# Attention of a fused two-block kernel: one pass per tile with a late combination, against two passes with the groups' weights put onto the exponents

## What is computed

```python
DILATION_CFG = ((128, 1), (512, 4), (2048, 16))

def dilated_window_attention(q, k, v, window, dilation):
    ...
    scores = jnp.where(valid[None, :, None, None], scores, -jnp.inf)
    m = jnp.max(scores, axis=-1, keepdims=True)
    p = jnp.exp(scores - m)
    den = jnp.sum(p, axis=-1)
    o = jnp.einsum('bnrhij,bnjrhd->bnirhd', p, vv)
    ...

def mixing_sublayer(h, cos, sin, w_in, w_pool, b_pool, pool_scale, w_out):
    ...
    alpha = jax.nn.softmax(jnp.stack(lses, axis=0), axis=0)
    attn = jnp.sum(alpha[..., None] * jnp.stack(outs, axis=0), axis=0)
    attn = attn.reshape(B, S, ATTN_OUT_WIDTH).astype(h.dtype)
    pool = causal_multiscale_pool(u_pool, w_pool, b_pool, pool_scale)
    return jnp.concatenate([pool, attn], axis=-1) @ w_out
```

## Time and profile before

| | |
|---|---|
| median of 3 runs | 1703.22 us (1702.44 to 1706.0) |
| the profiled execution, its own time | 1704.47 us |
| its span, first to last instruction | 1702.7 us |
| granted TensorE clock, mean | 0.957 |
| busy PE, PEld, DVE, ACT, POOL | 92%, 74%, 36%, 39%, 42% of the span |
| last transpose of the keys (end of the projection) | starts at 185.95 us |
| unit 10 of the output projection | starts at 277.69 us |

### The profile page before, as it was taken

One profiled execution on the slowest core, in us unless ns is written; L12 is line 12 of the kernel. 1 busy time (PEld: TensorE's weight loads), 2 busy tenths in 40 slices (PEclk: granted clock), 3 DMA queues, 4 the chain that ended last, 5 costly groups with the idle time before them and its releaser, 6 DMA issues.

```text
span 1702.7 us, 19973 instructions
## 1 busy us (share of the span) xinstructions
PE 1567.0 (92%) x7680; PEld 1264.1 (74%) x7680; DVE 610.5 (36%) x960; ACT 670.4 (39%) x1013; POOL 713.1 (42%) x608
## 2 busy tenths in 40 slices
PE   7899757799999999999988898999989999999996
PEld 4699534678888888878865567787878788887885
DVE  3665364433333300134024431243234455655001
ACT  2542452454444422332234354453333554554231
POOL 0466100344455444464421135334534445555442
PEclk8999886799999999999999998999999999999999
DMA  8463201512222233223311122222222222222221
GB/s 363 170 251 138 86 1 26 125 64 99 99 89 83 77 102 93 100 78 103 129 37 38 37 99 100 75 74 86 88 79 71 74 99 85 88 99 81 93 84 65
DMA packets 27148, 162.82 MB, mean 96 GB/s; under 512 B 3240, under 2 KB 3368, under 8 KB 12360
## 3 DMA queue, kind: packets, MB, share of 16 engines
q1 hardware_dynamic: 23616, 151.01, 25.9%
q10 hardware_dynamic: 3464, 10.88, 2.5%
HBM read 157.15 MB, written 4.72 MB: 95 GB/s over the span
## 4 chain that ended last, share of the span: by engine, by line
PE 68%; issue 10%; POOL 8%; DVE 7%; DMA 3%; ACT 3%; POOLq 0%; SPq 0%; ACTq 0%; DVEq 0%
PE ps L1624 58%; POOL WL L703 7%; DMA adaw<-w_ada_dram 2%; PE ps L1590 1%; PE ps L1835 1%; DMA raw<-w_up_dram 1%; PE ps L1849 1%; PE ps L1862 1%; DVE S L1515 1%; ACT S L906 1%; POOL WL L667 1%; DVE ps L1217 1%; PE ps L1789 1%; DVE S L1502 1%; DVE xT L1222 1%
## 5 line engine op out<-in xcount | busy, mean ns | idle before, releaser
L667 POOL TENSOR_TENSOR WL<-raw,WH 128x512 fp32r<-128x512 f32 (+2 forms) x344 | 368.9, 1101 | 621.0 <-ACT WH L783 620.9
L1624 PE MATMUL ps<-hH,WH 128*128 128x512 f32 x1136 | 461.1, 406 | 24.8 <-POOL hL L681 8.9
L1624 PE MATMUL ps<-hL,WH 128*128 128x512 f32 x1136 | 454.1, 400 | 0.0
L1624 PE MATMUL ps<-hH,WL 128*128 128x512 f32 x1136 | 453.9, 400 | 0.0
L703 POOL TENSOR_TENSOR WL<-raw,WH 128x512 fp32r<-128x512 f32 x176 | 246.2, 1431 | 254.1 <-ACT WH L931 254.1
L1624 PEld LDWEIGHTS ps<-hH,WH 128*128 128x128 f32 x1136 | 216.7, 191 | 83.6 <-issue 29.3
L1624 PEld LDWEIGHTS ps<-hH,WL 128*128 128x128 f32 x1136 | 216.5, 191 | 52.9
L1624 PEld LDWEIGHTS ps<-hL,WH 128*128 128x128 f32 x1136 | 216.9, 191 | 50.5
L783 ACT ACTIVATE WH<-raw 128x1024 fp32r<-128x1024 f32 (+3 forms) x172 | 148.1, 885 | 235.0 <-PE ps L1624 231.3
L1624 PE MATMUL ps<-hidH,WH 128*128 128x512 f32 x352 | 137.9, 392 | 1.1 <-POOL WL L703 1.1
L1624 PE MATMUL ps<-hidL,WH 128*128 128x512 f32 x352 | 137.0, 389 | 0.0
(11 more groups left out here) (269 smaller groups left out, 2268.4 us busy)
## 6 DMA issues: line engine op xcount, KB each, us to landing
raw<-w_up_dram SPq DMA_DIRECT2D x44, 1024.0 KB, 4.9
raw<-w_in_dram SPq DMA_DIRECT2D x36, 1024.0 KB, 4.9
adaw<-w_ada_dram SPq DMA_DIRECT2D x20, 1024.0 KB, 7.2
raw<-w_down_dram SPq DMA_DIRECT2D x16, 768.0 KB, 4.2
raw<-w_down_dram SPq DMA_DIRECT2D x16, 640.0 KB, 3.9
adap<-w_ada_dram SPq DMA_DIRECT2D x4, 1024.0 KB, 18.2
xT<-x_dram ACTq DMA_DIRECT2D x2, 2048.0 KB, 10.8
raw<-w_mem_kv_dram SPq DMA_DIRECT2D x4, 1024.0 KB, 4.8
```

The lines of the kernel that those rows point to most:

```text
L667: pool.tensor_tensor(WL[:, d % 2, ks, cols], raw[:, d % 2, ks, cols], WH[:, d % 2, ks, cols].bitcast(F32), ALU.subtract).then_inc(lo_done, 1)
L1624: mm = pe.matmul(out, lhs[x], rhs[y], start=(first and i == 0), stop=(last and i == 2))
```

## The change

The attention is rearranged into two passes.

First pass: all tiles' scores and exponents. Tiles 0 to 4 stand in the list between the projection's units 8 and 9 and their halves, the rest behind it. The mask is no longer added by DVE: TensorE puts it into the bank first, as a product of an fp32r identity with a mask table, and adds the scores to it. Tiles use two pairs of banks in turn, (4, 5) and (6, 7). DVE takes the maxima from PSUM. For tiles 5, 7, 9 and 11 (`WHOLE_EXP`) DVE then subtracts the maximum from all four heads at once, ACT takes one exponent of 512 elements, and DVE sums it (`tile_sum`); for the others ACT takes four exponents from PSUM with their sums. All exponents stay in `S1`.

Then the weights: maxima and sums stand with the queries on partitions, 48 of each. Those of group 0 (`md0`, contiguous queries) are brought into the order of the other groups by a store to DRAM and a load, and group 0's weights go back the same way (`al0`), four small transfers on SP's queue. DVE multiplies each tile's exponents with its weights (`scale`), first the eight tiles of groups 1 and 2, then group 0.

Second pass: 15 key blocks (`SUM_BLOCKS`), each four transposes, an ACT copy and four products with `V1`, all added up in banks 4 and 5 from a start of zeros. The steps `combine` and the copies to `oT` and `stats` are gone; the result is cut into `hH` and `hL` from PSUM (`attn_out`). The ACT and DVE part of `pool` is now `pool_out`, after key blocks 3 and 7. The cut of unit 11 (`split`) is behind the weights. Below are the tables, the list, the helpers, and then SP, ACT, DVE and TensorE.

```diff
 TILES1 = [(g, b, 2 if g == 0 and b > 0 else 1) for g in range(GROUPS) for b in range(TT)]
+NEAR = TT
+WHOLE_EXP = (5, 7, 9, 11)
+SCORE_BANKS = [((4, 5), (6, 7))[i] for i in (0, 1, 0, 0, 1, 0, 1, 0, 1, 0, 1, 0)]
+SUM_ORDER = list(range(NEAR, len(TILES1))) + list(range(NEAR))
+SUM_BLOCKS = [(n, kb) for n in SUM_ORDER for kb in range(TILES1[n][2])]
...
+            if d == ADA_REST:
+                steps += [("ada_end", 2)]
+            if d >= ADA_REST:
+                steps += [("front", 3 * (d - ADA_REST)), ("front", 3 * (d - ADA_REST) + 1)]
...
                 steps += [("trig",)]
             steps += [("seg", d, 1), ("evac_in", d)]
             if d == 3:
-                steps += [("spread_lo",)]
-            steps += [("split", d + 2)]
+                steps += [("spread_lo",), ("masks",)]
+            if d < D_OUT - 1:
+                steps += [("split", d + 2)]
+            if d == ADA_REST:
+                steps += [("front", 2)]
             if d < 3:
                 steps += [("spread_hi", k) for k in range(3 * d, min(3 * d + 3, KD))]
             if d in (1, 2, 4, 5):
...
-        steps += [("ada_end", 2), ("front", 0), ("pool",), ("front", 1)]
-        for n in range(len(TILES1)):
-            steps += [("mid", n)]
-            if n + 2 < len(TILES1):
-                steps += [("front", n + 2)]
-            steps += [("back", n)]
-        steps += [("combine",), ("bias_fetch",)]
+        steps += [("front", 5), ("pool",)] + [("front", n) for n in range(6, len(TILES1))] + [("weights",), ("split", D_OUT + 1)]
+        steps += [("scale", n) for n in SUM_ORDER] + [("mid", 0)]
+        for i in range(len(SUM_BLOCKS)):
+            if i + 1 < len(SUM_BLOCKS):
+                steps += [("mid", i + 1)]
+            steps += [("back", i)]
+            if i in (3, 7):
+                steps += [("pool_out", i // 4)]
+        steps += [("attn_out",), ("bias_fetch",)]
...
+        def scores(n):
+            nk, i = TILES1[n][2], key_blocks(n)
+            t = S1z[:] if n == len(TILES1) - 1 else S1[:, i:i + nk, :]
+            return t.rearrange("p k c -> p (k c)").rearrange("p (x w) -> p x w", x=GH)
+        def score_psum(n, x):
+            w = P * TILES1[n][2]
+            return ps[:, SCORE_BANKS[n][x // 2], w * (x % 2):w * (x % 2) + w]
+        def scores_read(eng, n):
+            if n in WHOLE_EXP:
+                eng.wait_ge(less_max, WHOLE_EXP.index(n) + 1)
+            else:
+                eng.wait_ge(exp_done, exps_before(n + 1))
...
-            dense(D_OUT, D_UP1)
+            dense(D_OUT, D_OUT + 3)
+            sp.wait_ge(negm_ready, NEAR)
+            sp.wait_ge(exp_done, exps_before(NEAR))
+            sp.dma_start(near_stats.ap().rearrange("(b p) c -> p b c", p=P), md0[:].rearrange("p b i h -> p b (i h)")
+                         ).then_inc(near_stored, 16)
+            sp.wait_ge(near_stored, 16)
+            sp.dma_start(mdj[:, 0, :, :, :].rearrange("p b i h -> p (b i h)"), near_stats.ap().rearrange("(p r) c -> p (r c)", r=TT)
+                         ).then_inc(near_loaded, 16)
+            sp.wait_ge(alpha_ready, 1)
+            sp.dma_start(near_weights.ap().rearrange("(p r) h -> p (r h)", r=TT), al[:, 0, :, :].rearrange("p b h -> p (b h)")
+                         ).then_inc(weights_stored, 16)
+            sp.wait_ge(weights_stored, 16)
+            sp.dma_start(al0[:], near_weights.ap().rearrange("(b p) h -> p b h", p=P)).then_inc(weights_loaded, 16)
+            load(D_OUT + 3)
...
             def front(n):
-                sc.wait_ge(negm_ready, n + 1)
-                w = P * TILES1[n][2]
+                t = scores(n)
+                if n == 0:
+                    sc.wait_ge(ada_turned, len(ADA_DVE))
+                if n in WHOLE_EXP:
+                    sc.wait_ge(less_max, WHOLE_EXP.index(n) + 1)
+                    sc.activation(t, t, ACT.Exp, scale=DH ** -0.5).then_inc(exp_done, 1)
+                    return
+                sc.wait_ge(negm_ready, n + 1 - sum(1 for i in WHOLE_EXP if i < n))
                 for x in range(GH):
-                    t = S1[:, n % 2, x // 2, x % 2, 0:w]
-                    sc.activation(t, t, ACT.Exp, bias=negm[:, n, x:x + 1], scale=DH ** -0.5,
...
+                    sc.activation(t[:, x, :], score_psum(n, x), ACT.Exp, bias=negm[:, n, x:x + 1], scale=DH ** -0.5,
+                                  accum_out=tile_stats(n)[:, 1, x:x + 1]).then_inc(exp_done, 1)
+            def weights():
                 sc.wait_ge(gap_ready, 1)
-                sc.activation(alpha[:], alpha[:], ACT.Exp, scale=DH ** -0.5).then_inc(gap_exp, 1)
-                for hp in range(2):
-                    sc.wait_ge(attn_ready, hp + 1)
-                    sc.activation(hH[:, 2 + hp, :], comb[:, 0, :], ACT.Copy).then_inc(cat_hi, 1)
+                sc.activation(al[:], al[:], ACT.Exp, scale=DH ** -0.5).then_inc(gap_exp, 1)
+            def mid(i):
+                sc.wait_ge(pt_done, i + 1)
+                if i >= 4:
+                    sc.wait_ge(pv_done, i - 3)
+                sc.activation(PT1[:, i % 4, :], ps[:, 6 + i % 2, :], ACT.Copy).then_inc(pt_read, 1)
+            def attn_out():
+                for q in range(2):
+                    sc.wait_ge(o_ready, q + 1)
+                    sc.activation(hH[:, 2 + q, :], ps[:, 4 + q, :], ACT.Copy).then_inc(cat_hi, 1)
...
+            def tile_sum(n):
+                ve.wait_ge(exp_done, exps_before(n + 1))
+                ve.tensor_reduce(tile_stats(n)[:, 1, :], scores(n), X, ALU.add).then_inc(far_summed, 1)
             def front(n):
+                nk = TILES1[n][2]
+                ve.wait_ge(s_done, 2 * n + 2)
+                top = tile_stats(n)[:, 0, :]
+                first, second = SCORE_BANKS[n]
+                src = ps[:, first:second + 1, 0:2 * P * nk].rearrange("p e (q w) -> p e q w", q=2)
+                link(ve.tensor_reduce(top.rearrange("p (e q) -> p e q", e=2), src, X, ALU.max))
+                if n in WHOLE_EXP:
+                    ve.tensor_tensor(scores(n).rearrange("p (e q) w -> p e q w", e=2), src,
+                                     top.rearrange("p (e q) -> p e q", e=2).unsqueeze(3).broadcast_to([P, 2, 2, P]), ALU.subtract
+                                     ).then_inc(less_max, 1)
+                else:
+                    ve.tensor_scalar(negm[:, n, :], top, -DH ** -0.5, None, ALU.mult).then_inc(negm_ready, 1)
+                if n - 1 in WHOLE_EXP:
+                    tile_sum(n - 1)
+            def weights():
+                tile_sum(WHOLE_EXP[-1])
+                ve.wait_ge(far_summed, len(WHOLE_EXP))
+                ve.wait_ge(near_loaded, 16)
+                top, total = mdj[:, :, :, 0, :], mdj[:, :, :, 1, :]
+                link(ve.tensor_reduce(mx[:], over_groups(top), X, ALU.max))
+                ve.tensor_tensor(al[:], top, over_all(mx[:]), ALU.subtract).then_inc(gap_ready, 1)
+                ve.wait_ge(gap_exp, 1)
+                link(ve.tensor_tensor(wt[:], al[:], total, ALU.mult))
+                link(ve.tensor_reduce(den[:], over_groups(wt[:]), X, ALU.add))
+                link(ve.reciprocal(rden[:], den[:]))
+                ve.tensor_tensor(al[:], al[:], over_all(rden[:]), ALU.mult).then_inc(alpha_ready, 1)
+                ve.wait_ge(alpha_ready, 1)
+            def scale(n):
...
+                if n == 0:
+                    ve.wait_ge(weights_loaded, 16)
+                w = al0[:, b, :] if n < NEAR else al[:, g, b, :]
+                ve.tensor_tensor(scores(n), scores(n), w.unsqueeze(2).broadcast_to([P, GH, P * nk]), ALU.mult).then_inc(p_scaled, 1)
+            def attn_out():
+                for q in range(2):
+                    ve.wait_ge(cat_hi, 3 + q)
+                    ve.tensor_tensor(hL[:, 2 + q, :], ps[:, 4 + q, :], hH[:, 2 + q, :].bitcast(F32), ALU.subtract
                                      ).then_inc(cat_lo, 1)
...
             def turn(e):
                 pe.wait_ge(rope_done, 2 * e + 2)
+                if e >= 4:
+                    scores_read(pe, (1, 4)[e - 4])
...
+                pe.wait_ge(turn_read, 12 if n >= 6 else 10 if n == 4 else 4 * g + 4)
+                if n == 0:
+                    pe.wait_ge(masks_ready, 2)
+                    pe.wait_ge(mod_ready, 3)
+                before = [i for i in range(n) if SCORE_BANKS[i] == SCORE_BANKS[n]]
+                if before:
+                    scores_read(pe, before[-1])
+                first = 0 if nk == 2 else 2 * P if g == 2 else P
+                for bank in SCORE_BANKS[n]:
+                    pe.matmul(ps[:, bank, 0:2 * P * nk], ident_r[:],
+                              mask[:, first:first + P * nk].unsqueeze(1).broadcast_to([P, 2, P * nk]), start=True, stop=False)
+                k0 = P * (b + 1 - nk)
                 for q in range(2):
                     for e in range(2):
                         r = slice(64 * e, 64 * e + 64)
-                        mm = pe.matmul(ps[:, 4 + e, 256 * q:256 * q + P * nk], qT[r, 2 * g + q, P * b:P * b + P],
```

(30 more changed lines are left out.)

199 lines of the change are left out of this document (61 added, 138 removed).

## The result

The changed kernel took 1665.99 us (median of 4, 1664.66 to 1666.63) against 1703.37 us in the runs beside it: a ratio of 0.9778, 95% interval 0.9763 to 0.9792. The forecast was 1662.5 us, range 1655 to 1680. The profiled execution has a span of 1664.8 us against 1702.7, so 37.9 us have to be found.

What follows compares the result with a forecast made beforehand. TensorE bounds the whole kernel, but in the attention no engine is full and dependent steps wait on each other. Unit 10 38.7 us earlier plus 2.0 behind it gives 40.7: 1662.5 us, range 1655 to 1680.

Steps and rivals of the forecast that it cites:

- What is added to the projection: Tiles 0 to 4 add 6.4 us on TensorE, the `ada_end` wait 0.8; last `turn` starts at 193.2.
- Tiles 5 to 11: Behind the projection: `pool` 3.6 us, paired tiles 3.5 us a round, last round 6.2; ends at 211.7.
- Weights: Between the passes: small DVE and ACT operations with hand-overs take 1.9 us; first `scale` ends at 214.3.
- rival 3: One unseen cost: strided PSUM writes, DVE slowed beside POOL, or slower PSUM exponents; +5 to +10, 1670 us; chance 0.15.
- Second pass: 15 key blocks at 1.12 us, 16.8, plus zeros 0.5, slow clock 2.5 and pool copies 3.0; ends at 237.2.
- the slow start: Start of the second pass: TensorE comes in at the lower clock after little work, losing 2.5 us.
- the pooled rows: In the second pass, `pool_out` work in ACT's way shows 1.5 us twice, 3.0 in all.
- Round trips: Four small DRAM transfers of weights, hidden at 2.3 us each; covers 21.4 and 13.1 us.
- Rival 4: DRAM transfers delay DVE and the second pass; 18.8 us each eats all 40.7, 19.7 gives 1707; chance 0.01.
- Behind it: After the attention, unit 10 runs at full clock, 2.0 us more gain; later waits move along.
- rival 2: TensorE stays at 1.2 GHz from tile 6 to unit 10: +17.8, 1680 us; chance 0.08.
- rival 1: First pass stays at full clock and pool copies hide: 4 to 6 less, 1658 us; chance 0.15.

Runs made afterwards that it cites:

- the fill: Thirteen unread TensorE products added between tile 11's scores and the weights, against the changed kernel: 1662.48 us.
- the run with seven: Six more DRAM round trips of the near groups' weights before the load `scale` waits for, against the changed kernel: 1680.18 us, ratio 0.9869.
- unchanged kernel: The changed kernel without a further edit, run in three groups: 1665.99, 1668.48 and 1664.61 us.

## Why the prediction was right, step by step

| step | forecast | measured (first profile) |
|---|---|---|
| last `turn` starts | 193.2 | 194.08 in the timeline |
| sum of tile 11 ends | 211.7 | 212.05 |
| first `scale` ends | 214.3 | 215.37 |
| second pass, with its waits | 22.9 us | 23.0 us |
| unit 10 starts | 239.0 | 240.30 |
| its first 24 products | 5.8 | 7.39 |

- **What is added to the projection.** Forecast 7.2, measured 8.1. The term that was mis-sized most is the mask products: from start to start in the timeline two of 256 columns take 0.40 to 0.43 where 0.24 was reckoned from the product of 512 in the earlier trace rows, two of 512 0.56 to 0.66 for 0.48, so 2.6 us for 1.9. (In the dense stretch two products of 256 columns take 0.24, so the pair by itself was priced rightly; where one kind of product gives way to another it costs more, and why, no run shows.) The wait for `ada_end` costs 1.1 us for 0.8 (from `ada_turn` to the next product 1.93, before 0.81); small pieces add 0.2, and this execution came to `ada_turn` 0.3 sooner. Halves of units 8 and 9 are 5.73 to 5.77 from start to start, as before (5.74), so the five tiles' other work is hidden there.
- **Tiles 5 to 11.** `pool` takes 1.86 where the earlier trace rows has 3.6: those were eight instructions at the lower clock (0.52 granted in 190 to 193.4 us of the trace before). That gives 1.7 back, and the clock, at 0.50 from 204 on, takes most of it: a tile's scores take 1.16 and 1.21 instead of 0.65 to 0.69. The forecast had the low clock only in the last tile. Its path at the end is not the measured one either: it has DVE's queue (sum of 9, maximum of 11, subtraction) behind tile 10, 6.2 us from tile 10's scores on; measured it is TensorE, whose scores of tiles 10 and 11 take 3.85 us one behind the other while DVE waits 0.40 for them, 6.7 us in all. The end was off by only 0.35 us because these cancel: +1.0 from the projection and tile 5, -1.7 from `pool`, +0.6 in the two rounds, +0.5 at the end.
- **Weights.** L1436 and the first `scale` were stretched beside GpSimd's cutting, 0.8 us (shown by moving it). It is the part of rival 3 that came true, at 0.8 and not 5 to 10 us. The other part did not: products of groups 1 and 2, which write every fourth column of PSUM, take 0.59 like those of group 0. The Trainium skill (SBUF — State Buffer, section "Door 1: The DMA port swizzle") says that any non-contiguous access to PSUM slows matmuls down significantly; here it doesn't, and the measurement decides.
- **Second pass.** 23.0 us for 22.9, of which the slow start is 2 (1.5 came back with the fill, DVE's second `scale` covers the rest) and the pooled rows 2.3 for 3.0 (shown by moving them). That the sum meets the forecast is luck: a key block takes 1.17 us where 1.12 was reckoned, 0.8 over the 15, and TensorE waits 0.19 before the last products; together that is about what the slow start and the pooled rows were too high by (0.3 to 0.5 and 0.7).
- **Round trips.** Four transfers landed in 1.4 to 1.8 us, the estimate was 2.3; no engine waited for them. Rival 4's mechanism is real, with its cover of 13.1 us measured as 13.4, but it needs more trips than one: in the run with seven the third already landed too late, at 229.96. The forecast took its risk from a load of 160 KB in 2.3 us and one at the start in 19.7; the case that matters here is a load beside x's, which took 7.75 (with its store 9.1, still inside the cover).
- **Behind it.** Here the one step fails: "TensorE was dense until 2 us before, so unit 10 should run at the full clock: 7.81 - 5.79 = 2.0 us more". It ran at 0.63 and 0.52 of the clock in 240 to 244 us, and 0.4 us was gained. The forecast's own sum has two gaps in this pass, so by its own terms TensorE was not dense; it was busy 84% of 222 to 238 us. The unchanged kernel had 7.39, 5.85 and 7.29 in three profiles, so the step is not wrong every time: the forecast took for certain what comes out one way or the other from execution to execution. The Trainium skill (TensorE: Matmul & The Clock Gate, section "HAM oscillation") has a kernel in which waits between bursts of matmuls bring the throttled level back again and again; the forecast priced that only as rival 2, for the whole stretch, and not for this one place. That such a fall can come behind 1.88 us without work, with two gaps of 1.17 us before, is what these traces show, in 5 of 6.
- **Sum.** 37.4 + 0.4 = 37.8 us for 38.7 + 2.0 = 40.7. The 1.3 us in unit 10's start are the 0.9 of the projection (most of it the mask products), and the 0.8 of GpSimd less what `pool` and the rest gave back; the 1.6 are the clock. The time of the whole kernel alone could not have judged such terms: two executions of the changed kernel took 1658.3 us, the number of rival 1, and the one of them that was profiled has the same stretch (45.90).

## What to carry to other kernels

Price a rebuilt stretch by one mark at its end and build the sum by pieces: the terms here were off by up to 1.7 us each, with both signs, and the sum by 2.9 of 40.7. When a chain of dependent steps per tile is taken apart into passes, look at three things: the operation with two SBUF inputs on VectorE that now stands beside GpSimd, the foreign work in the queue of the engine that copies out of PSUM (two gaps of 1.17 us, gone when it moved), and the first tens of products after each gathering of vector work, which may run at half the clock. Then ask which part of the change pays. Here the replaced combination was worth 24.5 us by the marks, overlap with the projection 10 to 11, and letting different tiles stand on different engines, by itself, some 2.5.

## What the runs showed of the hardware that was not expected

- One program's executions differ by up to 12 us of 1665 in the sum (1658.27 to 1670.19) while the stretch from the last `turn` to unit 10 repeats within 0.2 us, with its clock falls at somewhat different places; single groups of eight matmuls took 0.89 or 1.71 us at the same place. A gain below 5 us is to be read from marks.
- A fall of the clock can come up behind less than 1 us without work: in one of twelve profiles (unit 11 cut early) behind the 0.97 us before tile 0, in the middle of the dense projection, for 1.55 us of loss.
- An 8 KB load beside a 2 MB load took 7.75 us, elsewhere in the same execution 1.8 to 1.9.
- GpSimd's operations are stretched as well as VectorE's where they meet: 3.67 us for four against 2.80.
